# The sine products of the rotary rotations moved from VectorE to GpSimd, each sum one step later

## What is computed

```python
def _rotate(x, cos, sin):
    x1, x2 = jnp.split(x, 2, axis=-1)
    return jnp.concatenate([x1 * cos - x2 * sin, x1 * sin + x2 * cos], axis=-1)

def apply_axial_rope(x, tables):
    cr, sr, cc, sc = tables
    xr, xc = jnp.split(x, 2, axis=-1)
    return jnp.concatenate([_rotate(xr, cr, sr), _rotate(xc, cc, sc)], axis=-1).astype(x.dtype)

# in even_mixer
dq_x = apply_axial_rope(dq_x, tab_da)    # 8 groups of 64 columns
dk_x = apply_axial_rope(dk_x, tab_da)    # 8 groups of 64 columns
qr_x = apply_axial_rope(qr_x, tab_mla)   # 4 heads of 64 columns
kr_x = apply_axial_rope(kr_x, tab_mla)   # 1 group of 64 columns
```

## Time and profile before

| | us |
|---|---|
| median of 3 executions | 2691.98 |
| lowest, highest | 2689.43, 2693.33 |
| the profiled execution | 2694.56 |
| its span in the trace | 2692.8 |

### The profile page before, as it was taken

How to read it: one execution, slowest core, us unless ns; L and a number is a source line. 1 busy time by engine, 2 the same in 40 slices (tenths; PEclk the granted TensorE clock), 3 DMA queues, 4 the chain that set the end, 5 groups by cost and what they waited for, 6 DMA issues and landing times. The chain is left out here.

```text
span 2692.8 us, 48602 instructions
## 1 busy us (share of the span) xinstructions
PE 2570.8 (95%) x16525; PEld 2219.0 (82%) x16525; DVE 1696.8 (63%) x2507; ACT 1258.8 (47%) x1798; POOL 174.6 (6%) x215
## 2 busy tenths in 40 slices
PE   8999999999999999999999998899999999898999
PEld 8998877889888888877788886687898887666898
DVE  4556676765465475867665667766666566765555
ACT  4445445444344345444454563454444344553443
POOL 1000000010010000000000201200000011100000
PEclk9999999999999999999999999999999999999999
DMA  7655455467576564555566535553455858426564
GB/s 231 219 180 155 142 177 176 169 213 262 184 226 215 189 210 132 157 159 193 179 194 183 157 103 160 177 165 95 157 173 187 259 161 223 142 94 217 190 187 134
DMA packets 276177, 479.67 MB, mean 178 GB/s; under 512 B 17616, under 2 KB 87320, under 8 KB 275872
## 3 DMA queue, kind: packets, MB, share of 16 engines
q1 hardware_dynamic: 265632, 445.24, 51.9%
q0 software_dynamic: 10304, 31.31, 3.8%
HBM read 475.33 MB, written 6.92 MB: 179 GB/s over the span
## 5 line engine op out<-in xcount | busy, mean ns | idle before, releaser
L122 DVE TENSOR_TENSOR wlo<-raw,whi 128x1024 fp32r<-128x1024 f32 (+3 forms) x786 | 912.2, 1172 | 733.2 <-ACT whi L163 612.4
L163 ACT ACTIVATE whi<-raw 128x1024 fp32r<-128x1024 f32 (+3 forms) x786 | 786.4, 1015 | 639.3 <-PE bank L171 470.7
L171 PE MATMUL bank<-xh,whi 128*128 128x256 f32 x2208 | 635.8, 288 | 13.6 <-DVE xk L128 7.1
L171 PE MATMUL bank<-xl,whi 128*128 128x256 f32 x2208 | 628.1, 284 | 0.0
L171 PE MATMUL bank<-xh,wlo 128*128 128x256 f32 x2208 | 628.0, 284 | 0.0
L171 PEld LDWEIGHTS bank<-xh,whi 128*128 128x128 f32 x2208 | 425.9, 193 | 29.2 <-issue 18.2
L171 PEld LDWEIGHTS bank<-xl,whi 128*128 128x128 f32 x2208 | 425.6, 193 | 1.1 <-issue 0.5
L171 PEld LDWEIGHTS bank<-xh,wlo 128*128 128x128 f32 x2208 | 425.4, 193 | 0.0
L171 PE MATMUL bank<-whi,xh 128*128 128x512 f32 (+2 forms) x632 | 257.4, 407 | 19.2 <-issue 6.8
L171 PE MATMUL bank<-whi,xl 128*128 128x512 f32 (+2 forms) x632 | 249.2, 394 | 0.0
L171 PE MATMUL bank<-wlo,xh 128*128 128x512 f32 (+2 forms) x632 | 248.6, 393 | 0.0
(11 more groups left out here) (432 smaller groups left out, 3870.4 us busy)
## 6 DMA issues: line engine op xcount, KB each, us to landing
raw<-in_ffn_w_in SPq DMA_DIRECT2D x280, 512.0 KB, 4.5
raw<-in_ffn_w_out SPq DMA_DIRECT2D x154, 512.0 KB, 4.5
raw<-in_w_mix_in SPq DMA_DIRECT2D x112, 512.0 KB, 3.6
raw<-in_mod_w SPq DMA_DIRECT2D x96, 512.0 KB, 4.9
raw<-in_od_w_in SPq DMA_DIRECT2D x40, 512.0 KB, 4.7
raw<-in_ffn_w_in SPq DMA_DIRECT2D x56, 256.0 KB, 2.9
raw<-in_w_branch SPq DMA_DIRECT2D x24, 512.0 KB, 3.6
raw<-in_ev_w_in SPq DMA_DIRECT2D x24, 512.0 KB, 4.1
```

Source lines behind the costliest of these rows:

```text
L122: return Made(self.e and self.e.tensor_tensor(out, a, b, op))
L163: return Made(self.e and self.e.activation(out, a, f, **k))
L171: return Made(self.e and self.e.matmul(out, lhs, rhs, **k))
```

## The change

The two products with the sine go to POOL, which waits for the same things as DVE did; a `yield` is put between the products and the sum. So a call of `rope` takes two ticks more.

```diff
         c = co.rt[:, table, t, 0:64].unsqueeze(1).to_broadcast([P, g, 64])
         co.dv.wait_ge(ready, free, co.gains)
         a = co.dv.tensor_tensor(w[:, t], v[:, t], c, ALU.mult).then_inc(co.s_dv)
+        co.po.wait_ge(ready, free, co.gains)
         for h in range(2):
             o = w2[:, t].rearrange("p g (a h n) -> p g a h n", a=2, h=2)[:, :, :, h]
             i = v[:, t].rearrange("p g (a h n) -> p g a h n", a=2, h=2)[:, :, :, 1 - h]
             s = co.rt[:, table, t, 64:128].rearrange("p (a h n) -> p a h n", a=2, h=2)[:, :, h].unsqueeze(1)\
                 .to_broadcast([P, g, 2, 16])
-            b = co.dv.tensor_tensor(o, i, s, ALU.mult).then_inc(co.s_dv)
+            b = co.po.tensor_tensor(o, i, s, ALU.mult).then_inc(co.s_po)
+        yield
         co.dv.wait_ge(a, b)
         out.append(co.dv.tensor_tensor(v[:, t], w[:, t], w2[:, t], ALU.add).then_inc(co.s_dv))
         if t == 0:
```

## The result

| | before | changed |
|---|---|---|
| median, us | 2692.61 | 2696.33 |
| lowest, highest | 2684.97, 2697.58 | 2693.22, 2702.08 |
| executions | 20 | 20 |
| the profiled execution, its span | 2694.56, 2692.8 | 2693.22, 2691.4 |

The ratio is 1.0017, interval 1.0010 to 1.0023. That is slower, by less than the 0.2% that the prediction called no change, and 8 us above the predicted 2688.1; the range ended at 2695.0. One execution of 5202 us in e10 and one of 5690 us of before beside it are left out of medians and ratios.)

A forecast was written before the change was run, and what follows sets the result against it. PE bounds the kernel, busy 2570.8 of 2692.8 us. Region -4.1, key columns 0, end of projections +0.3, given as -3.9 with rounding, took the median 2691.98 to 2688.1 us; range 2684.0 to 2695.0.

The forecast's parts named there:

- The order and the region: PE around dk's and dq's transposes: both two steps later, dq's wait gone, f4 at 1748.6; gain 4.1 us.
- The term of 1.34 us for the clock of q0's block: Behind dq's wait: q0's block took 3.52 us at lower clock, 2.18 at full clock; 1.34 us to win.
- The price of a product on POOL: One 128x256 sine product on POOL: estimated 0.94 us, bounds 0.38 and 2.05.
- Rival C: POOL's 256-column products and DVE hold each other up near dk's second pair: 2.1 us lost, 2690.2 us; chance 0.15.
- The first wait: Before dk's transposes: dk's second sine products stand behind dq's powers on POOL; wait not shortened, net loss 0.86 us.
- The key columns and the end of the projections: Key columns' sine products hidden by PE's matmuls, cost 0; last sum behind two DVE products, cost 0.3 us.
- The steps taken there are missing later beside PE's own blocks, so 0: Behind the projections: the modulation steps used up there were said to cost 0 later.
- the other parts: MLA queries 0, end of projections 0.3 us, steps missing later 0, DVE's saved 5 us worth 0.
- Rival B: Third score item: the 2.97 us wait on `px` goes too, items beginning behind the context's 16th block; 2685.1 us, chance 0.27.
- Cases in which a later part loses: Rival of costly POOL products holding DVE at the key columns: 2692.8 us at 2.05 each, 2700.7 at 4; chance 0.09.

The follow-up runs named there:

- e10: The changed kernel with the attention's marks taken early (e1) and dq's multiplication by its norm one step later; median 2695.39 us, ratio 1.0014 to the kernel before.
- e7: The changed kernel again, nothing edited; median 2698.07 us, ratio 1.0018 to the kernel before.
- e1: The changed kernel with the attention's marks taken as soon as x's projections are ready; median 2693.53 us, ratio 1.0005 to the kernel before.
- e2: The kernel before with only the added yield, sine products left on DVE; median 2693.8 us, ratio 1.0009 to the kernel before.
- e4: The kernel before with the added yield, sine products on DVE, and the attention's marks taken early; median 2693.0 us, ratio 0.9999 to the kernel before.
- e9: e4 with dq's multiplication by its norm one step later; median 2693.99 us, ratio 1.0006 to the kernel before.
- e3: The kernel before with only the sine products moved to POOL, no added yield; median 2696.78 us, ratio 1.0018 to the kernel before.
- e12: The same kernel as e5 once more: the kernel before with dq's transposes two ticks later; median 2687.92 us, ratio 0.9979 to the kernel before.
- e11: e12 with the sine products on POOL and no yield in the rotation; median 2693.96 us, ratio 1.0001 to the kernel before.
- e5: The kernel before with only dq's transposes two ticks later, rotations whole and on DVE; median 2688.63 us, ratio 0.9985 to the kernel before.
- e6: The kernel before with dk's row tiles rotated in one step, dk's transposes two and dq's three ticks later; median 2689.29 us, ratio 0.9990.

## Why the prediction was wrong, point by point

**The order and the region: right.** The order came as counted. On before's clock (5.97 us added) dk's transposes started at 1730.72, forecast 1730.25; dq's at 1743.17, forecast 1743.2, without a wait; f4 at 1747.97, forecast 1748.6. The region gained 4.8 us for the 4.1 said, and 2.8 and 2.9 in the two other profiles of the same code (e7, e1), in which dk's transposes came 1.8 and 1.7 us later behind dv. The term of 1.34 us for the clock of q0's block is confirmed: with no stop ahead of it the block took 2.17 us. (The terms of the sum give -3.8; the -3.9 of the forecast is a slip of 0.1.)

**The price of a product on POOL: a little high.** Tile `lb`, POOL's groups by form, and POOL's timeline of the changed kernel:

```profile
L122 POOL TENSOR_TENSOR lb<-etk,rtg 128x256 f32<-128x256 f32 x8 | 8.7, 1114 | 2.0 <-DVE etk L122 2.0
```

```profile
1718.10 3.61 POOL L122 TENSOR_TENSOR cst<-cst 128x8 f32<-128x8 f32 x2 [2.51 <-DVE cst L129]
1721.68 1.87 POOL L122 TENSOR_TENSOR lb<-etk,rtg 128x256 f32<-128x256 f32 x2
1724.78 3.99 POOL L122 TENSOR_TENSOR lb<-etk,rtg 128x256 f32<-128x256 f32 x2 [1.23 <-DVE etk L122]
...
1732.96 1.44 POOL L122 TENSOR_TENSOR lb<-etk,rtg 128x256 f32<-128x256 f32 x2
```

Undisturbed, two take 1.44 us, 0.72 each, against 0.94 taken and bounds of 0.38 and 2.05. DVE's took 0.38 (a pair 0.75): a ratio of 1.9. The Trainium skill (GPSIMD Engine Reference, Performance versus the Vector engine) gives 1.96 for a `tensor_tensor` add of 2048 float32 columns, and the trace agrees. The mean of 1.11 us comes from pairs beside DVE's work.

**Rival C was there, and was small.** DVE's timeline of the changed kernel at the same moment:

```profile
1721.74 1.21 DVE L122 TENSOR_TENSOR etk<-etk,cst 128x512 f32<-128x512 f32 x1 [0.91 <-POOL cst L122]
1722.88 1.22 DVE L122 TENSOR_TENSOR wlo<-raw,whi 128x512 fp32r<-128x512 f32 x1
```

Both take 0.68 to 0.69 us elsewhere. They are longer here, beside POOL's products of 256 columns; beside the powers of eight columns (1718.10 to 1721.71) DVE's 128x512 product at 1720.14 took 0.69, as the earlier trace rows had let one expect. The rule of the Trainium skill that was weighed there (SBUF — State Buffer, on who interferes with whom) holds here for POOL's products and is not visible for its powers. With a small product it is POOL that pays: one of 128x32, in the pair at 1681.03, took 1.28 us instead of 0.25 while DVE made a `wlo`. POOL's and DVE's timelines:

```profile
1681.03 1.49 POOL L122 TENSOR_TENSOR lb<-etk,rtg 128x32 f32<-128x32 f32 x2 [0.29 <-POOL lb L122]
```

```profile
1680.98 1.22 DVE L122 TENSOR_TENSOR wlo<-raw,whi 128x1024 fp32r<-128x1024 f32 x1
```

The longer DVE products are a part of why DVE's busy time fell by only 1.6 us when twenty products left it. Rival C put 2.1 us on this; dk's transposes were 0.5 us later than forecast.

**The first wait: right in kind, and it decides about the engine.** The prediction said that dk's second sine products would stand behind dq's powers, so that this wait would not be shortened. In the pairs that differ in the engine alone (with the steps: e2 to changed, e4 to e1, e9 to e10; without: before to e3, e12 to e11) it is longer on POOL by 1.1, 1.1, 2.8, 2.9 and 2.9 us, and the ratio is higher each time: by 0.06 to 0.08% in the three pairs with the steps, each less than the interval of one ratio, and by 0.18 and 0.22% in the two without. Moving the products helped nowhere.

**The key columns and the end of the projections: 0, where 0 and 0.3 were said.** Between dv and 1706 PE has no wait in the changed kernel, and none on the last transposes. The key columns' sum did wait for POOL, 2.9 of the 3.6 us of DVE's wait shown above, but in the shadow of PE's blocks; a product of 128x32 was cheaper than the 0.94 taken.

**The step that failed: "The steps taken there are missing later beside PE's own blocks, so 0".** And with it the account of "the other parts", which looked at DVE's saved products and at PE's cover, not at who else goes by the order. Two things were behind that 0:
- The *marks*. When `x` is ready two steps later, `ev.attend` takes `counts(co)` behind the issue of a load that it doesn't need. e1 and e4 show this by 5.1 and 4.9 us from dv to okt, 0.12 and 0.10% in the ratio. It also makes the wait on `px` last 5.60 us at once, with the granted clock at 0.50, the lower of TensorE's two levels (1.2 GHz), for the 4 us behind it, where it was 0.70 behind before's wait on `px`. Windows of the changed kernel and of before (busy us of PE, PEld, DVE, ACT, POOL; then granted clock, DMA share, GB/s):

```profile
1804.90:1808.90 4.00, 3.71 (x10) 1.74 (x11) 3.65 (x4) 1.76 (x3) 0.00 (x0) 0.50 0.27 63
```

```profile
1805.30:1809.30 4.00, 4.00 (x14) 2.59 (x15) 3.38 (x8) 2.11 (x5) 0.00 (x0) 0.70 0.30 79
```

- The *cover*. The context is four blocks ahead, and it is likely that these blocks are missing where `x`'s output rows are normed for the SwiGLU (`x2h`). PE's timeline of the changed kernel:

```profile
1989.60 0.36 PE L171 MATMUL bank<-ch,whi 128*128 128x256 f32 x1 [0.48 <-issue]
...
1994.03 0.36 PE L171 MATMUL bank<-x2h,whi 128*128 128x256 f32 x1 [2.78 <-issue]
```

Before has a wait there too, of 1.96 us. PE's waits from 200 to 560 us behind dv are 4.8 us before, 6.9 in the changed kernel, 7.5 in e1 and 5.8 in e4, with four blocks of lead, and 4.6 in e5 and 5.2 in e12 with two; but 8.8 in e6, with three. So the lead doesn't set them alone. That it is a cause is a guess from these, not shown by an edit of its own. What is shown is the size of the loss that stays behind the region when the marks are early: 2.7 us in e1 and 3.5 in e4 (what the region gained, 2.9 and 4.6, less the 0.2 and 1.1 left at the end), where the prediction had 0.3.

**Rival B had the place and the wrong sign.** The wait on `px` was named as what might go too, by moving behind the context's 16th block. The items did begin behind it, and what the context does there was looked at for its DVE products alone, not for its transfers. Cases in which a later part loses had 0.09, all of it for the key columns; the range reached up by that price and no further.

**The balance.** From dv to the end: -4.8 in the region, +9.3 behind it, +4.6 in all. PE's waits behind the region grew by 4.3 (95 to 200 us behind dv), 1.0 (to 350), 1.1 (to 560) and 2.2 (the rest, from 27.4 to 29.6; 29.1 in e7). With 0.4 between the region and 95 us that is 9.0 of the 9.3; the last 0.3 was not traced.

## What to carry to other kernels

An added step is not local where a program's order is decided by "who is ready": follow it to every place at which someone takes a snapshot of all marks (`counts`, "all that was issued so far"), and see which transfers are now inside. Take such a mark when what it stands for becomes true, not when it is used. A gap can be closed where it is (two steps ahead of one product's transposes, 0.15 and 0.21% faster) without moving an engine's work; and before work goes to an idle engine, look at what stands in its queue at that moment: POOL was 7% busy and had 3.6 us of powers ahead at the one place that mattered.

## What the runs showed of the hardware

- A POOL product of 128x256 takes 0.72 us; two of them took 3.99 us (from 1724.78) beside three DVE operations with two inputs in SBUF, `wlo` of 1024 columns at 1724.62 and 1726.96 (1.21 us each) and the cosine product at 1726.36 (0.67). Here POOL alone paid, 2.55 us; DVE's three took what they take elsewhere.
- Small products are no dearer on POOL than large ones, against DVE: of eight of 128x64 seven take 0.32 to 0.33 us, where DVE took 0.22, and of four of 128x32 three take 0.25, where DVE took 0.18, ratios of 1.5 and 1.4 against 1.9 for 128x256. The eighth and the fourth took 1.30 and 1.28, each beside a `wlo` of DVE; the mean of 0.45 us for 128x64 hides this.
- The same code, from the start to dv, took 1673.6 to 1681.3 us in the fourteen profiles. For a change of 5 us the common instruction near the edit is the zero, not the start of the span.
